# The source of three relative-position tables: 128 partitions or one per head, and an earlier wait for their stores

## The reference, cut to what matters

```python
# sliding window attention, 16 heads
bias = rel_bias[bucket]                 # rel_bias (32, 16), bucket from t + 128 - s
bias = bias.transpose(2, 0, 1)          # per head, (128, 256)
logits = jnp.einsum('bqhgd,bkhd->bhgqk', qn, kn) * scale + bias
...
# chunk attention, 8 heads
bias = rel_table[:, jnp.clip(rel, -128, 128) + 128]
s = jnp.einsum('bcqhd,bckhd->bhcqk', qc, kb) * (64 ** -0.5) + bias[:, None]
```

## Time and profile before

| | |
|---|---|
| median of 3 runs | 3572.24 us (3569.57 to 3572.83) |
| profiled execution | 3572.83 us, span 3571.0 us |
| mean granted TensorE clock | 0.987 |
| busy in the span: TensorE, VectorE, ScalarE, GpSimd | 97%, 49%, 26%, 61% |
| store of the chunk rows, issue to landing | 12.9 us |
| store of the window rows, issue to landing | 24.8 us |

### The profile page before, as it was taken

The page is one execution under the profiler, slowest core; times in us unless marked ns, Lnnn a source line. Parts: engine busy times, 40 slices in busy tenths (PEclk is TensorE's granted clock), DMA queues, the critical chain, the costliest instruction groups (busy, mean ns, idle before and its releaser), DMA issues. The chain is left out here.

```text
span 3571.0 us, 45392 instructions
## 1 busy us (share of the span) xinstructions
PE 3468.6 (97%) x16406; PEld 2826.0 (79%) x16406; DVE 1734.3 (49%) x3381; ACT 932.9 (26%) x1613; POOL 2184.7 (61%) x2180
## 2 busy tenths in 40 slices
PE   7998999998899999999999999999999999999998
PEld 5775888886578888877788877788888888888887
DVE  6563444246654433427423766645555244444443
ACT  3354222123532211125421111133333211111111
POOL 5421766774256667664357776755554578878885
PEclk9998999999899999999999999999999999999999
DMA  6110222222022222221222233334444565555552
GB/s 204 59 36 24 92 103 95 95 95 83 24 72 100 95 95 95 100 90 52 77 71 95 106 137 139 127 148 186 189 180 183 207 228 189 188 191 198 194 198 91
DMA packets 134328, 440.17 MB, mean 123 GB/s; under 512 B 7139, under 2 KB 76932, under 8 KB 97284
## 3 DMA queue, kind: packets, MB, share of 16 engines
q1 hardware_dynamic: 39168, 285.23, 22.4%
q10 hardware_dynamic: 94980, 152.40, 12.1%
HBM read 362.64 MB, written 74.96 MB: 123 GB/s over the span
## 5 line engine op out<-in xcount | busy, mean ns | idle before, releaser
L192 PE MATMUL banks<-memory,weights_split 128*128 128x512 f32 x9456 | 2254.2, 396 | 38.5 <-DMA memory<-in_consts 16.8
L192 PEld LDWEIGHTS banks<-memory,weights_split 128*128 128x128 f32 x9456 | 1764.4, 189 | 435.9 <-issue 53.5
L2982 POOL TENSOR_SCALAR weights_split<-weights_raw 128x512 fp32r<-128x512 f32 x1088 | 744.3, 694 | 1363.0 <-PE banks L192 692.4
L2987 POOL TENSOR_TENSOR weights_split<-weights_raw,weights_split 128x512 fp32r<-128x512 f32 x1088 | 1490.1, 1381 | 0.0
L192 PE MATMUL banks<-weights_split,memory 128*128 128x512 f32 (+1 forms) x3648 | 822.2, 387 | 1.9 <-DVE memory L1365 1.9
L192 PEld LDWEIGHTS banks<-weights_split,memory 128*128 128x128 f32 x3648 | 679.1, 188 | 141.4 <-DVE memory L1365 2.3
L2744 DVE TENSOR_TENSOR memory<-memory,memory 128x512 fp32r<-128x512 f32 x128 | 167.4, 1308 | 353.7 <-ACT memory L2858 353.7
L2723 DVE TENSOR_SCALAR memory<-banks,memory 128x128 f32<-128x128 f32 x512 | 174.3, 402 | 214.0 <-PE banks L2590 205.0
L2858 ACT ACTIVATE memory<-memory 128x512 fp32r<-128x512 f32 x128 | 80.8, 632 | 601.0 <-PE banks L192 587.3
L2791 ACT ACTIVATE memory<-banks 128x512 f32<-128x512 f32 x128 | 76.6, 598 | 569.2 <-PE banks L192 569.2
L2738 DVE TENSOR_TENSOR memory<-memory,memory 128x512 f32<-128x512 f32 x128 | 166.3, 1300 | 51.2 <-DMA memory<-hidden 44.7
(11 more groups left out here) (243 smaller groups left out, 2257.2 us busy)
## 6 DMA issues: line engine op xcount, KB each, us to landing
weights_raw<-in_weights SPq DMA_DIRECT2D x272, 1024.0 KB, 4.8
hidden<-memory ACTq DMA_DIRECT2D x64, 512.0 KB, 2.7
routing<-memory ACTq DMA_DIRECT2D x16, 2048.0 KB, 6.3
memory<-routing ACTq DMA_DIRECT2D x32, 1024.0 KB, 8.2
memory<-hidden ACTq DMA_DIRECT2D x32, 1024.0 KB, 10.4
window_rows<-memory ACTq DMA_DIRECT2D x1, 3064.0 KB, 24.8
chunk_rows<-memory ACTq DMA_DIRECT2D x1, 2556.0 KB, 12.9
residual<-in_x ACTq DMA_DIRECT2D x4, 512.0 KB, 11.0
```

Source lines behind the costliest of these rows:

```text
L192: last = k.nc.tensor.matmul(out, left[a], right[b], start=start and n == 0, stop=stop and n == 2, skip_group_check=True)
L2982: k.nc.gpsimd.tensor_scalar(cut(high, n * PIECE, PIECE), cut(raw, n * PIECE, PIECE), 1.0, 1.0, ALU.mult, ALU.mult).then_inc(k.high_made, 1)
L2987: k.nc.gpsimd.tensor_tensor(cut(low, n * PIECE, PIECE), cut(raw, n * PIECE, PIECE), cut(high, n * PIECE, PIECE).bitcast(F32), ALU.subtract ...
```

## The change

The rows are built on one partition per head (8 and 16 partitions) instead of on 128. The chunk rows are stored by one DMA that reads 8 partitions, each 128 times. The window rows are stored by four DMAs, each from four partitions, each read 128 times; the first has the place of the former store, the other three stand behind the first three Silus. ScalarE's wait for all five stores moves from tick 9 to the place ahead of tick 0. The chunk table is loaded once instead of repeated 16 times, and the columns are 16 wide for `rel_bias` instead of 128.

```diff
-                     sinks=SW_HEADS, lambdas=4 * 64, rel_bias=P)
+                     sinks=SW_HEADS, lambdas=4 * 64, rel_bias=SW_HEADS)
...
-    STORES = 2
+    STORES = 5
...
-        act.dma_start(self.table, k.dram["chunk_table"].unsqueeze(1).broadcast_to(
-            [CH_HEADS, P // CH_HEADS, 2 * REL_CLIP + 1])).then_inc(self.loaded, 16)
+        act.dma_start(self.table[0:CH_HEADS, :], k.dram["chunk_table"]).then_inc(self.loaded, 16)
...
-        k.nc.tensor.matmul(self.bank.memory[:, 0:BUCKET_ROWS], k.column("rel_bias")[0:BUCKETS + 1, :],
+        k.nc.tensor.matmul(self.bank.memory[0:SW_HEADS, 0:BUCKET_ROWS], k.column("rel_bias")[0:BUCKETS + 1, :],
                            self.buckets[0:BUCKETS + 1, :], start=True, stop=True).then_inc(k.filled, 1)
...
-        v.tensor_scalar(chunk_rows[:, 0:flat], table[:, 0:1].broadcast_to([P, flat]), -1.0, None,
-                        ALU.mult).then_inc(self.built, 1)
-        v.tensor_scalar(chunk_rows[:, flat:], table[:, 0:TOKENS + P - 1 - flat], -1.0, None,
+        v.tensor_scalar(chunk_rows[0:CH_HEADS, 0:flat], table[0:CH_HEADS, 0:1].broadcast_to([CH_HEADS, flat]), -1.0,
+                        None, ALU.mult).then_inc(self.built, 1)
+        v.tensor_scalar(chunk_rows[0:CH_HEADS, flat:], table[0:CH_HEADS, 0:TOKENS + P - 1 - flat], -1.0, None,
                         ALU.mult).then_inc(self.built, 1)
         self.bank.await_filled(dve)
-        v.tensor_scalar(self.rows, self.bank.memory[:, 0:BUCKET_ROWS], -1.0, None,
+        v.tensor_scalar(self.rows[0:SW_HEADS, :], self.bank.memory[0:SW_HEADS, 0:BUCKET_ROWS], -1.0, None,
                         ALU.mult).then_inc(k.freed["vector"], 1)
...
         if n == 0:
             act.wait_ge(self.built, 2)
-            rows, heads, width, to = self.chunk_rows, CH_HEADS, TOKENS + P - 1, k.dram["chunk_rows"]
-        else:
+            act.dma_start(k.dram["chunk_rows"], self.chunk_rows[0:CH_HEADS, :].unsqueeze(1).broadcast_to(
+                [CH_HEADS, P, TOKENS + P - 1])).then_inc(self.written, 16)
+            return
+        if n == 1:
             self.bank.await_read(act)
-            rows, heads, width, to = self.rows, SW_HEADS, BUCKET_ROWS, k.dram["window_rows"]
-        act.dma_start(to.rearrange("h (r j) u -> (h r) j u", j=heads),
-                      rows.unsqueeze(1).broadcast_to([P, heads, width])).then_inc(self.written, 16)
+        heads = slice(4 * (n - 1), 4 * n)
+        act.dma_start(k.dram["window_rows"][heads], self.rows[heads, :].unsqueeze(1).broadcast_to(
+            [4, P, BUCKET_ROWS])).then_inc(self.written, 16)
...
             made[4 + n].await_read(act)
             a.activation(queries_b[n], queries_b[n], ACT.Silu).then_inc(silu_q, 1)
+            if n < 3:
+                rows.store(act, 2 + n)
+        rows.await_written(act)
         for t in range(LAST + 1):
...
-            if t == STICK_AT:
-                rows.await_written(act)
...
-    c["rel_bias"] = np.repeat(np.concatenate([a["rel_bias"], np.ones((P - BUCKETS, SW_HEADS), np.float32)]),
-                              P // SW_HEADS, axis=1)
+    c["rel_bias"] = np.concatenate([a["rel_bias"], np.ones((P - BUCKETS, SW_HEADS), np.float32)])
```

## The result

The changed kernel takes 3704.86 us (median of 4 runs, 3699.48 to 3706.77) against 3571.21 us of the kernel before beside it (4 runs): ratio 1.0372, 95% interval 1.0354 to 1.0390. It is slower by 134 us; the forecast was 3704. The profiled execution took 3700.36 us, with a span of 3698.6 us and a mean granted clock of 0.971.

The account below looks back on a forecast made before the run. TensorE, with a matmul in flight in 97% of the span, was taken to bound the kernel. Landing 227 - 98.3 = 128.7, + 3 for the clock - 0.15 for loads = 131.5 us on 3572.83: 3704, range 3586 to 3735 (0.8).

Parts of the forecast that it names:

- engine pace: Rival A: narrow stores' engines share no path, 22.0 GB/s each; landing 120.5, 3598 us (3586 to 3620); chance 0.33.
- one shared path for four neighbours: Store sources: four neighbouring partitions together give 25.9 GB/s; stores take 171.7 us, landing at 227; chance 0.47.
- The landing: Last store lands at 227 us; room up to 98.3, beyond which each microsecond is one on TensorE: 128.7 us.
- Four engines: Each window store, with outermost dimension 4, runs on four DMA engines instead of 16; DMA share near 0.25.
- The cross product of tick 2: TensorE stalls at this product from 101.4 us, through ScalarE's exponents behind the moved wait, until landing + 3.1 us.
- the table load: ScalarE's load ahead of its exponents, put behind the moved wait: 1.28 us between landing and TensorE's resumption.
- the clock: Granted clock falls after TensorE's long idling; 3 us of work lost.
- C: Rival, slower still: narrow stores hold ScalarE at issue or delay weight packets, doubled slots still fitting; no chance of its own given.
- The held issues: Narrow stores hold ScalarE at their issue; while it waits anyway, at most 5.7 us through a late cross product.
- the 46 us named for the move: ScalarE's wait moved from tick 9: free landing up to about 144 us becomes 98.3, taking away 46 us of room.
- The smaller loads: Loads ahead of TensorE's start shrink, columns by 56 KB; gain 0.15 us, 0 to 0.3.
- VectorE's long copy: Copy (1.44 us) keeps its columns and loses partitions; effect on the time taken as 0.

Follow-up runs that it names:

- e3: Changed kernel with each window store reading heads n, n+4, n+8, n+12 instead of four neighbours; 3622.21 us, ratio 1.0150.
- e7: Changed kernel with each window store's heads four apart and the chunk rows on partitions 0, 4, ... 28; 3590.03 us against 3570.08 before.
- e1: Changed kernel with only ScalarE's wait for the stores put back at tick 9; 3657.28 us (one run) against 3569.22 before.
- e2: Kernel before with only ScalarE's wait moved ahead of tick 0, stores still from 128 partitions; 3568.30 us, ratio 1.0002.
- e6: Changed kernel with the chunk rows on 128 partitions again, window stores still from four neighbours; 3656.52 us against 3570.08 before.

## Why the prediction was right

*The path.* The step on which all hung was the choice between engine pace and one shared path for four neighbours. e3 shows it: the same DMAs on four groups run at 90 instead of 26 GB/s. The chosen rate, the fastest load row's 25.9 per engine, was near: 26 to 27 was measured, and 50 for the chunk rows' two groups. The landing came at 226.2 (forecast 227), by two small errors that nearly cancelled: from the first issue the stores took 173.8 us instead of 171.7, and that issue stood at 52.40 us instead of 55.3.

*Four engines.* The share of 0.23 to 0.27, and 22.5 GB/s for each of four in e3, fit the split over as many engines as there are source partitions. The rule of the Trainium skill (DMA: Bandwidth & Descriptors, "Why a DMA increments its semaphore by 16 and not by 1") agrees; which engines they were no run shows.

*The place and length of the stall.* The cross product of tick 2 was the instruction, as said, and each microsecond of landing beyond about 98 was one of time: from e7 to e3 to the changed kernel the first exponent moves by 34.7 and 77.2 us, and the span (3588.2, 3622.5, 3698.6 us) by 34.3 and 76.1. The added time can be read from two places. The cross product of tick 2 started at 227.76 us and not at 101.62, 126.1 us later. The low clock after the gap cost 1.4 us by the windows (0.1 from 227.76 to 228, 0.50 x 2, 0.16 x 2). Together that is 127.5 of the span's 127.6. The forecast was 131.5, some 4 us high, and its three larger errors point the same way: the table load (1.28 us) stood ahead of the wait and not behind it, so TensorE resumed 1.6 us after the landing instead of 3.1; the landing was 0.8 early; and the clock was put at 3.

So the mechanism was right, but the match to a microsecond is luck. The profiled executions differ by 127.5 us and the medians by 133.65, one below the forecast's 131.5 and one above it, and the changed kernel's runs alone lie between 3699.48 and 3706.77.

*The weights.* One step of the prediction was too mild: under C the text said that a weight slot's landing, if doubled, still fits. The four slots issued from 56 to 104 us took 21.6, 14.0, 20.1 and 14.0 us, two to three times the 6.8 of the earlier trace rows, and GpSimd waited 11.0 us for one. Its waits from 60 to 120 us (total, times, longest):

```profile
POOL weights_split L2984 <- DMA weights_raw<-in_weights: 11.0, 1, 11.0
```

TensorE then lost 5.8 us ahead of the loop, where it had lost 1.9. With the opening 2.6 us ahead of before's in this profile (chunk store issued at 52.40 us, 54.99 in the earlier trace rows) this is why the stall began at 103.67 us and not at 101.4. That start adds nothing to the total: the stall ends with the landing, so what comes late ahead of it only makes the stall shorter. The earlier opening is scatter: over the runs above this issue lies between 52.4 and 55.2 us. It counts only in that it moves the stores, and so the landing, with it.

*The held issues.* The text allowed for them and gave them at most 5.7 us. They lasted far longer (119 us together) and cost nothing here, since ScalarE had only the landing to wait for and the first Silu (78.86) was still ahead of the diagonal cross product (97.84). With the wait at tick 9 they are what TensorE waits for (e1): the 46 us named for the move came out, but by chance. The prediction had counted to a landing that tick 9 could still wait for (144 us); the runs show the end of the last held issue (181 us in e1) against the landing at about 226.

*The small terms.* The smaller loads were to start TensorE 0.15 us earlier; it started at 16.93 us (16.84 in the earlier trace rows), so no gain shows. VectorE's long copy took 1.44 us on 8 partitions as on 128 (group of the changed kernel, 40 to 88 us: busy, mean ns, idle):

```profile
L850 DVE TENSOR_SCALAR memory<-memory 8x383 f32<-8x383 f32 x1 | 1.4, 1441 | 0.0
```

## What to carry to other kernels

A store's pace is set by where its source lies, not only by its bytes: count its source partitions along the outermost dimension (here they set the number of engines) and the paths that these partitions lie on, and take the smaller. The same 3.1 MB ran at 26, 55 and 90 GB/s from four partitions on one, two and four paths. Repeating a row over all partitions on the compute engines cost next to nothing here (the long copy took 1.44 us on 8 partitions and on 128), and it frees the store. And a wait that is moved ahead costs nothing as long as the landing is early (e2): price the landing first, then the wait.

## What the runs showed of the hardware that was not expected

Issuing a DMA is not always short: with much of the earlier stores still to move on the same engines, an issue on ScalarE's queue held it for 17.9 to 38.9 us, where it takes 0.5 otherwise. The held times follow the pace of the earlier stores: 9.3 to 12.4 us in e7 (behind a first of 0.6), 7.7 to 34.9 in e3. That the queue takes only so many rows for each engine is an inference; its depth was not measured.

Stores that crawl also hold up the loads of another queue. With the chunk rows on two groups a weight slot took 14.0 to 21.6 us, though the total DMA share was only 0.5 to 0.65. In e7, with as many source partitions on groups of their own and a like share, it took 7.3 to 8.8 us; in the kernel before 4.8 to 11.8. In e6, with only the window rows on one group, two of four slots took 16.4 and 17.5 us. How the engines divide their time between the two queues was not measured.
